# Second mixer's entry built from transposed rows, the second layer's end read out of PSUM, and the last down piece taken by contraction halves

## What is computed

```
def rms_norm(x, gain):
    y = xf * lax.rsqrt(jnp.mean(xf * xf, axis=-1, keepdims=True) + NORM_EPS)
    return (y * gain.astype(jnp.float32)).astype(x.dtype)
...
def hier_moe(h, ...):
    ...
    for e in range(N_EXPERTS):
        hid = jax.nn.silu(hf @ w_gate[e]) * (hf @ w_up[e])
        y = y + (hid @ w_down[e]) * combine[:, e:e + 1]
...
    for layer in range(DEPTH):
        ...
            p = rms_norm(h, o_norm[i]) @ o_w_in[i]
            h = h + gla_mix(p, o_g_up[i], o_g_b[i], o_head_gain[i]) @ o_w_out[i]
        h = h + hier_moe(rms_norm(h, m_norm[layer]), ...)
    return rms_norm(h[:, N_META:], final_norm)
```

## Time and profile before

| | us |
|---|---|
| median of 3 runs | 851.76 |
| lowest and highest | 851.48, 852.13 |
| the profiled execution's own time | 853.37 |
| its span, first to last instruction | 851.70 |
| PE busy in the span | 761.6 |
| DVE busy, ACT busy | 327.3, 206.2 |

### The profile page before, as it was taken

The page is one execution under the profiler, slowest core; times in us unless marked ns, Lnnn a source line. Parts: engine busy times, 40 slices in busy tenths (PEclk is TensorE's granted clock), DMA queues, the critical chain, the costliest instruction groups (busy, mean ns, idle before and its releaser), DMA issues.

```text
span 851.7 us, 16959 instructions
## 1 busy us (share of the span) xinstructions
PE 761.6 (89%) x7570; PEld 512.5 (60%) x7570; DVE 327.3 (38%) x689; ACT 206.2 (24%) x419; POOL 12.8 (2%) x62
## 2 busy tenths in 40 slices
PE   8999999899998988899888999999999968766875
PEld 6879777775765546555444878886575544333422
DVE  4566855453336332233335125543242512112213
ACT  3663245421500000000004163452041000000003
POOL 6000000000000000000000000000000000000000
PEclk9999999999999999999999999999999989889888
DMA  8543000506999999999999644003999999999994
GB/s 268 171 116 101 2 3 2 200 2 277 421 416 421 421 419 421 421 411 416 421 403 350 221 126 146 2 2 130 372 387 371 421 422 421 419 421 421 421 412 175
DMA packets 65383, 242.08 MB, mean 284 GB/s; under 512 B 9606, under 2 KB 33276, under 8 KB 42396
## 3 DMA queue, kind: packets, MB, share of 16 engines
q1 hardware_dynamic: 65244, 240.94, 72.0%
q10 hardware_dynamic: 64, 0.02, 0.0%
HBM read 239.90 MB, written 1.05 MB: 283 GB/s over the span
## 4 chain that ended last, share of the span: by engine, by line
PE 75%; DMA 13%; DVE 4%; SPq 3%; issue 2%; ACT 2%; PEldq 0%; POOL 0%; ACTq 0%; DVEq 0%; POOLq 0%
PE ps L1448 11%; PE ps L1211 11%; PE ps L882 10%; PE ps L1166 7%; PE ps L1081 7%; DMA M<-in_m_w_down_dram 5%; PE ps L1250 4%; DMA M<-in_m_w_up_dram 4%; DMA M<-in_m_w_gate_dram 4%; PE ps L1181 4%; SPq L356 3%; PE ps L1033 2%; PE ps L1002 2%; PE ps L838 2%; DVE H L1931 2%
## 5 line engine op out<-in xcount | busy, mean ns | idle before, releaser
L1211 PE MATMUL ps<-M 128*32 128x256 f32 x2016 | 127.0, 404 | 35.0 <-DMA M<-in_m_w_gate_dram 29.2
L1211 PEld LDWEIGHTS ps<-M 128*32 128x32 f32 x2016 | 70.4, 116 | 98.1 <-DMA M<-in_m_w_gate_dram 33.7
L1448 PE MATMUL ps<-M 128*128 128x256 f32 (+2 forms) x400 | 91.2, 385 | 1.0 <-DVE M L1580 1.0
L882 PE MATMUL ps<-M 128*128 128x272 f32 x352 | 88.4, 401 | 1.6 <-DVE M L1580 1.0
L1448 PEld LDWEIGHTS ps<-M 128*128 128x128 f32 (+1 forms) x400 | 73.3, 186 | 15.9 <-issue 3.5
L1166 PE MATMUL ps<-M 128*128 128x128 f32 x688 | 80.3, 276 | 0.0
L1166 PEld LDWEIGHTS ps<-M 128*128 128x128 f32 x688 | 78.3, 192 | 1.8 <-issue 1.8
L882 PEld LDWEIGHTS ps<-M 128*128 128x128 f32 x352 | 64.5, 190 | 16.3 <-issue 2.4
L1928 DVE TENSOR_TENSOR H<-H,ps 128x512 f32<-128x512 f32 x60 | 41.3, 688 | 83.7 <-PE ps L1181 83.5
L1181 PE MATMUL ps<-M 128*128 128x512 f32 x120 | 60.3, 624 | 8.4 <-DVE H L1931 6.0
L1250 PE MATMUL ps<-M 128*32 128x512 f32 x448 | 52.4, 609 | 11.4 <-DMA M<-in_m_w_down_dram 6.7
(11 more groups left out here) (382 smaller groups left out, 856.3 us busy)
## 6 DMA issues: line engine op xcount, KB each, us to landing
M<-in_m_w_gate_dram SPq DMA_DIRECT2D x32, 2048.0 KB, 15.9
M<-in_m_w_up_dram SPq DMA_DIRECT2D x28, 2048.0 KB, 21.7
M<-in_m_w_down_dram SPq DMA_DIRECT2D x28, 2048.0 KB, 22.0
M<-in_o_w_in_dram SPq DMA_DIRECT2D x12, 1024.0 KB, 5.5
M<-in_e_w_in_dram SPq DMA_DIRECT2D x11, 1024.0 KB, 5.4
M<-in_m_w_down_dram SPq DMA_DIRECT2D x9, 1024.0 KB, 20.7
M<-in_m_w_up_dram SPq DMA_DIRECT2D x5, 1024.0 KB, 8.2
M<-in_e_w_out_dram SPq DMA_DIRECT2D x1, 4096.0 KB, 13.9
```

The source lines that it names most:

```text
L882: ins = pe.matmul(ps[:, n % 4, 0:T], wringE[:, (n // 2) % 4, k, (n % 2) * P:(n % 2) * P + P], xnE[:, k], start=(k == 0), stop=(k == KD - 1))
L1211: ins = pe.matmul(ps[32 * e:32 * e + 32, 3 * x, 0:FF], xgT[q % 2][:, k, 32 * e:32 * e + 32], w, start=(k == 0), stop=(k == KD - 1))
L1448: ins = pe.matmul(ps[rows, unit % 4, 0:n], lhs(k), rhs(k), start=(k == 0), stop=(k == KD - 1))
```

## The change

Four things are rewritten. (1) At the boundary, `H` is no longer transposed after the last group was added. `old_rows(k)` multiplies slice k of `H` (before the last group) with the identity into PSUM; `new_rows(k)` adds the last group's contribution, already transposed, to the same PSUM columns as a product of `yst` and `RTL` (the last group's routing weights). ACT squares these transposed rows (`squared_rows`), PE sums the squares over the partitions by matmuls with one column of ones (`row_sums`, `meta_sums`), ACT takes the roots, DVE inverts them and scales the identity three times in one instruction, one matmul spreads them, and DVE makes `xnO` out of PSUM. The additions to `H` are still made, two of them after `xnO`. (2) The first projection and the first half of the second are interleaved step by step. (3) In the last group of layer 0 the up unit is done in halves with two and three of the `combined` products ahead of each; its transfer is split to fit. (4) The last down piece is taken by contraction halves, in both layers; at the end `H`'s right half is put into PSUM with a product of the identity, the last group is added there, and squares and the final product read PSUM. Row tile 1 of the output is stored from ACT's queue.

```diff
+                        elif u == NU - 2 and y == 0:
+                            if h == 0:
+                                sp.dma_start(slots[j][:, :, 0:D], up[:, 4 * q:4 * q + 4, 0:D]).then_inc(s("ld_half"), 16)
+                            else:
+                                for e in (0, 2):
+                                    sp.dma_start(slots[j][:, e:e + 2, D:2 * D], up[:, 4 * q + e:4 * q + e + 2, D:2 * D]) \
+                                        .then_inc(s(f"ld_s{j}"), 16)
...
+                    if q == NQ - 1:
+                        warm_up(ACT.Sqrt)
...
+            squared_rows(0)
+            squared_rows(2)
+            act.wait_ge(s("dn_last"), 1)
+            nc.scalar.activation(yst[1][:, 768:D], ps[:, 3, 0:256], ACT.Copy).then_inc(s("yl"), 1)
+            squared_rows(4)
+            squared_rows(6)
...
+                def old_rows(k):
+
+                    at_k = k % 2 * SEQ
+                    for t in range(2):
+                        pe.matmul(ps[:, 4 + k // 2, at_k + t * P:at_k + t * P + P], H[:, t, k * P:(k + 1) * P], ident[:, :],
+                                  start=(k % 2 == 0 and t == 0), stop=False, skip_group_check=True)
+                    pe.matmul(ps[:, 2, META * k:META * k + META], H[:, 2, k * P:(k + 1) * P], ident[:, 0:META],
+                              start=(k == 4), stop=False, skip_group_check=True)
+
+                def new_rows(k):
+
+                    at_k, ys = k % 2 * SEQ, yst[(NQ - 1) % 2][:, k * P:(k + 1) * P]
+                    pe.matmul(ps[:, 4 + k // 2, at_k:at_k + SEQ], ys, RTL[:, META:T], start=False, stop=True, skip_group_check=True)
+                    pe.matmul(ps[:, 2, META * k:META * k + META], ys, RTL[:, 0:META], start=False, stop=True,
+                              skip_group_check=True).then_inc(s("entry_pe"), 1)
+
+                def row_sums(k, n_act):
+
+                    pe.wait_ge(s("entry_act"), 3 + n_act)
+                    for x in range(2):
+                        for t in range(2):
+                            o = x * SEQ + t * P
+                            pe.matmul(ps[:, 3, 384 + t:385 + t], sqT[k // 2][:, o:o + P], ones[:, 0:1], start=(k + x + t == 0),
+                                      stop=(k + x == KD - 1), skip_group_check=True)
...
+                    if q == NQ - 1 and y == 0:
+                        combined(q - 1, (0, 1))
+                        pe.wait_ge(s("ld_half"), 80)
+                        half_gu(3 * q + 1, q, 1, range(0, 4))
+                        combined(q - 1, range(2, nu))
+                        loaded(3 * q + 1)
+                        half_gu(3 * q + 1, q, 1, range(4, KD))
...
+                    if q == NQ - 1 and y == 0:
+                        pe.wait_ge(s("rt_set"), n + 1)
+                        for k in (4, 5, 6, 7, 0, 1):
+                            old_rows(k)
...
+                if y == 0:
+                    pe.wait_ge(s("ld_last0"), 32)
+                    last_down(0, 512, 1).then_inc(s("dn_done"), 1)
+                    for k in (2, 3):
+                        old_rows(k)
+                    pe.wait_ge(s("ya"), n + 1)
+                    for k in range(4):
+                        new_rows(k)
+                    last_combine(0, 0, 0)
+                    last_combine(2, 0, 1)
+                    row_sums(0, 1)
+                    row_sums(2, 2)
+                    pe.wait_ge(s("ld_lastk"), 16)
+                    pe.wait_ge(s("acc"), at0 + 1)
+                    last_down(512, 256, 0, (0,))
+                    last_down(768, 256, 3, (0,), first=False)
+                    pe.wait_ge(s("ld_last1"), 16)
+                    last_down(512, 256, 0, (1,)).then_inc(s("dn_done"), 1)
+                    last_down(768, 256, 3, (1,)).then_inc(s("dn_last"), 1)
+                    pe.wait_ge(s("acc"), at0 + 2)
+                    last_combine(1, 0, 1)
+                    pe.wait_ge(s("yd"), n + 1)
+                    new_rows(4)
+                    new_rows(5)
+                    pe.wait_ge(s("yl"), 1)
+                    new_rows(6)
+                    new_rows(7)
...
+                    row_sums(4, 3)
+                    row_sums(6, 4)
+                    meta_sums().then_inc(s("entry_pe"), 1)
+                    pe.wait_ge(s("acc"), at0 + 3)
+                    last_combine(0, 1, 1)
+                    pe.wait_ge(s("entry_dve"), 3 + 1)
+                    last_combine(2, 1, 2)
+                    pe.wait_ge(s("entry_dve"), 3 + 2)
+                    pe.matmul(ps[:, 0, 0:T], ones[:, :], diagO.rearrange("p t c -> p (t c)")[:, 0:T], start=True, stop=True) \
+                        .then_inc(s("entry_pe"), 1)
+                    last_combine(1, 1, 3)
+                    return
+                pe.wait_ge(s("acc"), at0)
+                for t in range(2):
+                    pe.matmul(ps[:, 1 + t, :], ident[:, :], H[:, t, 512:D], start=True, stop=False)
-                if y == 0:
-                    row_turn(2, range(4))
-                    row_turn(0, range(4))
-                    row_turn(1, range(4))
...
+                for t in range(2):
+                    pe.matmul(ps[:, 1 + t, :], rt_[:, TOK[t]], ys[:, 512:D], start=False, stop=True).then_inc(s("cb"), 1)
...
+                    tt(diagO, ident[:, :].unsqueeze(1).to_broadcast([P, 3, P]), rs[:, 2, :].unsqueeze(2).to_broadcast([P, 3, P]), ALU.mult) \
+                        .then_inc(s("entry_dve"), 1)
```

262 lines of the change are left out of this document (139 added, 123 removed).

## The result

The changed kernel takes **864.19 us** (median of 4 executions, 862.28 to 867.54), where the one before took 851.94 beside it (4 executions, 851.48 to 853.92): a ratio of 1.0143, with a 95% interval of 1.0107 to 1.018. Forecast were 858.5 and at most 861.3. The direction was right, the size was not.

A forecast was written before the change was run, and what follows sets the result against it. PE was taken to bound the kernel at the boundary, whose delay moves everything behind it. The first projection comes 6.5 us later and the end adds 0.2: 851.76 + 6.5 + 0.2 = 858.5 us, range 855.3 to 861.3.

The forecast's parts named there:

- What bounds the kernel: At the boundary PE is the filled engine; any gain or loss there moves second mixer, weight stream and end equally.
- Halves of up: Layer 0's last up unit: its first half fills PE's wait for DVE's additions, up ends at 445.6, gain 1.1 us.
- The boundary's PE work: From old_rows at 447.2 to the end of meta_sums at 467.3: PE works without a pause, 20.1 us together.
- The choice between 0.04 and 0.107: Boundary row sums, 32 passes with one moving column: priced at 0.107 a pass, 3.4 us; lower bound 0.04, 1.3.
- The figure that the forecast kept as a rival: Boundary row sums by the skill's 25 ns issue gap: 0.8 us, kernel at 855.9; shares the 0.07 chance.
- The tail: Chain from meta_sums to the first projection: 3.4 us, ending at 470.7, with three last_combine under it.
- The interleaving: First two projection units: interleaving gains nothing; a step's two products cost 0.46 each, PE sets the pace.
- The end: Last down piece, norm and stores: second store net 0.2 us later, bounds 0.8 earlier and 0.6 later.
- Few moving columns: Rival at the boundary: row sums run at 0.04 a pass, 2.1 us off, 856.4; chance 0.07.
- narrow products: Rival: passes with at most 16 moving columns hide under neighbours, 7.5 us off, 851.0; chance 0.04.
- The second mixer: Rival: it waits for transfers issued at a fixed time and absorbs half the delay, 855; chance 0.03.
- The waits: Rival: a dozen hand-overs between PE and ACT or DVE cost 0.2 more each, 2.4 us, 861; chance 0.10.

The follow-up runs named there:

- a_no_interleave: The changed kernel with the first two projection units one after the other again, not interleaved: 862.60 us, ratio 1.0115.
- b_interleave: The kernel before with the step-by-step interleaving of the first two projection units alone: 854.0 us beside 851.96, ratio 1.0018.
- b_end: The kernel before with the change's end of layer 1 alone, second store from ACT's queue: 852.55 us beside 851.83, ratio 1.0000.
- the last version: The kernel before with layer 0's last up unit in halves and the PSUM end reordered, both stores from SP: 850.13 us beside 851.83, ratio 0.9975.
- the best set: The changed kernel unaltered, six executions beside 23 of the kernel before: 863.65 us against 851.83, ratio 1.0129.
- the second: The changed kernel unaltered, run again beside the kernel before: 866.04 us against 851.96, ratio 1.0179.

## Why the prediction came out too low

**What bounds the kernel: right.** What the boundary loses moves all that follows. PE was busy in all of the stretch that the forecast gave to it, the landmark at layer 1 moved by 10.3, and the stretch behind it by -0.7. That -0.7 is no gain of the change: in the five kernels with the old end the same stretch is 260.40 to 261.64.

**Halves of up: right in kind, 0.4 too much.** -0.7 instead of -1.1. The sum added passes as if a change of the weights' width were free, and each of the two changes that the halves add costs 0.15; it gave the three products 2.7 where they take 2.96 in either kernel; against that, the 0.1 of wait that it allowed did not come.

**The boundary's PE work: 20.1 forecast, 21.1 measured.** By the starts of its pieces: the row sums 1.87 and 1.85 for 3.4, 0.116 a pass (+0.3); the down pieces 1.85 and 1.87 for 1.72 each, again at changes of width (+0.3); the old rows 5.5 for 5.1 (+0.4); the combines 2.5 for 2.2 (+0.3); the new rows 5.2 for 5.3 (-0.1); `meta_sums` 0.48 for 0.6 (-0.1). The choice between 0.04 and 0.107 for one moving column was right, and so was the reason: the load of 128 weight columns sets the pace. The Trainium skill states that price in "TensorE: Matmul & The Clock Gate", section LDWEIGHTS (loading the stationary operand): nanoseconds about the number of weight columns over 1.2, so 107 for 128, and the traces' 0.107 to 0.119 agree. The figure that the forecast kept as a rival, from the section Back-to-back issue gap of the same page, 25 ns for 1 to 64 moving columns, does not come out with such a load ahead of each pass: the traces show 0.116 at one column and 0.119 at 64. With 16 weight columns and one moving column they show 0.03.

**The tail: 3.4 forecast, 3.63 measured.** One link was hidden wrongly: DVE's scaled identity is done at 474.59, but the spread starts at 474.88, right behind the meta rows' `last_combine` that the forecast had put under the chain. Together with the two terms above, the first projection came 8.2 later instead of 6.5.

**The interleaving: the step that failed.** The prediction read 0.22 a pass from 49 passes, took 0.46 for each product of a step, 0.92 in all, in any order, and added that "PE set the pace before and sets it now". PE does set it, but at 1.19 a step. The order of the products is part of their price, and the row it was read from had only one change of width in it. That one change can be seen in the trace of the kernel before, in the weight loads of the same 49 passes, which stand open once:

```profile
467.94 6.12 PEld L1448 LDWEIGHTS ps<-M 128*128 128x128 f32 x29 [0.45 <-issue]
```

This is +2.1, the largest single error; leaving the interleaving out gives 2.1 back by the landmark (a_no_interleave), and putting it in costs 1.8 (b_interleave). The forecast gave it no bound at all, which is why the range was too narrow: with the 1.7 at the boundary it makes 3.8 of the 5.7 by which the median missed. (The bounds that the prediction lists add up to 862.0, not 861.3, and would not have held 864.19 either.)

**The end: a small error, with two false steps that partly cancel.** Forecast +0.2; measured +0.6 from the last up product to the end of the span. The first two `last_combine` came 1.9 later, not 1.0 (the prediction's own terms, 1.8 in a pause of 0.6 and 0.9 more, add up to 2.1), and the last two products 1.5 later, not 0.6. The identity products were given a pause of 0.6, but they stand behind the very wait that makes the pause. Behind the last two products 0.4 came back up to DVE's second final product, as forecast: the addition is gone, and the scaling on DVE took 0.48 (given 0.45). Another 0.5 came back behind that product, and this was luck. Its start before, and then its start and the issue of the second store after:

```profile
846.85 0.75 DVE L2161 SCALAR_TENSOR_TENSOR M<-H,rs 128x512 f32<-128x512 f32 x1
```

```profile
861.51 0.75 DVE L2267 SCALAR_TENSOR_TENSOR M<-ps,rs,H 128x512 f32<-128x512 f32 x1
...
862.31 0.39 ACTq L796 DMA_DIRECT2D out_dram<-M  x1
```

From there to the end of the span it is 4.80 before and 4.31 after. b_end, with ACT's queue as the issuer, has 4.31 again, and the last version, with both stores from SP and both scalings on ACT, 4.80. So ACT's queue as the issuer, together with the scaling moved to DVE, is worth 0.5, where the prediction gave it zero. The two are not told apart, and a last version with them was not run.

**The rivals.** Few moving columns are not cheap, and narrow products don't hide: the row sums took 1.87 and 1.85. The second mixer absorbed nothing. The waits didn't add up at the boundary either; 861 was the number nearest to the result, for another reason.

**What stays open.** By the landmarks the change costs 9.6 to 9.8 from G to the end in all three of its traces, against the one trace of the kernel before (10.0 with the mean of the five stretches behind layer 1 named above, 261.1); the medians differ by 11.8 in the best set, 12.3 in the first and 14.1 in the second. The intervals of the first and the best set (9.1 to 15.3, 8.9 to 13.1) hold 9.7, that of the second (12.5 to 18.1) does not. Part of the surplus goes with the clock. Each execution lists its mean granted clock over the span. At 0.977 and 0.978 the changed kernel has a median of 862.59 (7 executions) and the one before 851.83 (31), 10.8 apart. At 0.976 and below lie 6 of 14 executions of the changed kernel, at 865.07 to 870.64, but only 10 of 49 of the one before. One such execution has a trace, the first, and its clock was low in the first projection and once more between 172 and 175, both ahead of the boundary. Whether the change makes such executions more frequent, and where the clock falls in the others, is not shown; nor where the last 1 us lies.

## What to carry over

Price a small product by its weight load, and price a sequence by its changes of weight width too: keep products of one width together, and interleave only equal widths. Before work is said to fill a pause, find the wait that makes the pause and look on which side of it the work is queued. Products that accumulate in PSUM spare DVE its additions, but they are paid on PE: here some 11 us (old rows 5.5 for 3.5, new rows 5.2, sums 4.2) on the engine that was already full.

## What the runs showed of the hardware

- **A change of the weights' width leaves the load uncovered.** Between 16 and 128 columns it costs 0.15 to 0.17 for each change, between 128 and 32 the rows show about 0.15; an alternation of equal widths cost 0.04 in all. The Trainium skill's "TensorE: Matmul & The Clock Gate", section Step-by-step: what each phase is for, says that PE pulls weight loads ahead of running products, where the rows of the array do not conflict or the load goes to the background buffer. The rows agree where the width stays (the load of L1254 at 459.81 starts 0.2 ahead of its product at 460.02, under the one before) and not where it changes: at 477.45 and 478.65 the load starts with its product.
- **One, 16 and 64 moving columns cost nearly the same**, 0.107 to 0.119 a pass with 128 weight columns; with 16 weight columns it was 0.03.
- **The same program can get another clock.** It began its first projection at 12.28 and got 0.65 and 0.67 of the clock in the stretches 10 to 15 and 15 to 20, or at 11.43 and got all of it: 3.0 us for the same 32 passes. And the variant with 5.5 us of PE work taken away at the boundary had a stretch at 0.50 right behind it, which took 2.3 of the gain back.
